# Two-block model on one core: the experts' gate and up products as three one-pass products of split operands, down weights loaded whole

## What is computed

```python
def hierarchical_moe(h, rg_w, rg_b, re_w, re_b, w_gate, w_up, w_down):
    ...  # combine[token, expert]: weight of the two chosen experts, else 0
    for e in range(N_EXPERTS):                                   # 16
        act = jax.nn.silu(hf @ w_gate[e]) * (hf @ w_up[e])       # 512x1024 @ 1024x512
        out = out + combine[:, e:e + 1] * (act @ w_down[e])      # 512x512 @ 512x1024
    return out.reshape(b, s, d)

def first_block(...):
    ...
    h2 = rmsnorm(x, norm2_g[l]) * (1.0 + scale2) + shift2
    y = hierarchical_moe(h2, ...)
    x = x + gate2 * y
    return rmsnorm(x, final_g)
```

## Time and profile before

| | us |
|---|---|
| median of 3 runs | 2555.88 |
| lowest to highest | 2555.7 to 2556.81 |
| the profiled execution | 2549.77 |
| its span in the trace | 2548.2 |

### The profile page before, as it was taken

One profiled execution on the slowest core, in us unless ns is written; L12 is line 12 of the kernel. 1 busy time (PEld: TensorE's weight loads), 2 busy tenths in 40 slices (PEclk: granted clock), 3 DMA queues, 4 the chain that ended last, 5 costly groups with the idle time before them and its releaser, 6 DMA issues.

```text
span 2548.2 us, 25617 instructions
## 1 busy us (share of the span) xinstructions
PE 2320.7 (91%) x9884; PEld 1662.4 (65%) x9884; DVE 1069.1 (42%) x1528; ACT 787.8 (31%) x1292; POOL 180.5 (7%) x222
## 2 busy tenths in 40 slices
PE   6899999979999995988879999989999997899998
PEld 4657666654444444874668888878865555788887
DVE  5635533351111115224554444453335544544444
ACT  3444521231010013210542123442344553311343
POOL 0330002010000001001000000001212200000000
PEclk9999899999999997978989999999989998999999
DMA  9304035728988884302023222233100001232221
GB/s 355 108 1 149 17 110 180 273 83 297 316 302 311 308 302 140 99 21 78 1 66 97 94 99 99 100 84 111 56 2 1 1 1 53 88 99 93 90 100 66
DMA packets 156367, 309.23 MB, mean 121 GB/s; under 512 B 18014, under 2 KB 19939, under 8 KB 156261
## 3 DMA queue, kind: packets, MB, share of 16 engines
q1 hardware_dynamic: 136308, 261.21, 30.2%
q0 software_dynamic: 11376, 41.42, 4.2%
q10 hardware_dynamic: 8580, 5.16, 0.8%
HBM read 276.56 MB, written 30.99 MB: 121 GB/s over the span
## 4 chain that ended last, share of the span: by engine, by line
PE 79%; DVE 10%; ACT 4%; issue 3%; DMA 2%; ACTq 1%; POOL 0%; DVEq 0%; POOLq 0%; SPq 0%; PEldq 0%
PE PB L1530 45%; PE PB L1933 8%; PE PB L1952 4%; PE PB L2212 3%; PE PB L1515 2%; PE PB L2188 1%; DVE WL L2306 1%; PE PB L1993 1%; PE PB L2016 1%; PE PB L2189 1%; DVE CI L3028 1%; PE PB L1756 1%; PE PB L2151 1%; DVE X L2366 1%; PE PB L1677 1%
## 5 line engine op out<-in xcount | busy, mean ns | idle before, releaser
L2306 DVE TENSOR_TENSOR WL<-RING,WH 128x1024 fp32r<-128x1024 f32 x232 | 286.3, 1234 | 662.0 <-ACT WH L892 385.6
L892 ACT CAST WH<-RING 128x1024 fp32r<-128x1024 f32 x232 | 243.4, 1049 | 873.8 <-PE PB L1530 849.2
L1530 PE MATMUL PB<-HTH,WH 128*128 128x512 f32 x1056 | 416.6, 395 | 16.0 <-DVE WL L2306 10.2
L1530 PE MATMUL PB<-HTL,WH 128*128 128x512 f32 x1056 | 413.8, 392 | 0.0
L1530 PE MATMUL PB<-HTH,WL 128*128 128x512 f32 x1056 | 413.2, 391 | 0.0
L1530 PEld LDWEIGHTS PB<-HTH,WH 128*128 128x128 f32 x1056 | 200.0, 189 | 61.8 <-DVE WL L2306 12.5
L1933 PE MATMUL PB<-RING,HT 128*128 128x512 f32 x512 | 226.3, 600 | 9.0 <-DVE HT L2782 5.7
L1530 PEld LDWEIGHTS PB<-HTH,WL 128*128 128x128 f32 x1056 | 199.9, 189 | 41.9
L1530 PEld LDWEIGHTS PB<-HTL,WH 128*128 128x128 f32 x1056 | 200.1, 190 | 41.5 <-issue 0.7
L1530 PE MATMUL PB<-WH,NHH 128*128 128x512 f32 x512 | 199.4, 389 | 1.8 <-DVE NHL L2309 1.8
L1530 PE MATMUL PB<-WH,NHL 128*128 128x512 f32 x512 | 199.2, 389 | 0.0
(11 more groups left out here) (489 smaller groups left out, 3266.0 us busy)
## 6 DMA issues: line engine op xcount, KB each, us to landing
RING<-in_mlp_w SPq DMA_DIRECT2D x64, 1024.0 KB, 5.1
RING<-in_expert_w_gate SPq DMA_DIRECT2D x32, 1024.0 KB, 5.5
RING<-in_expert_w_up SPq DMA_DIRECT2D x32, 1024.0 KB, 5.7
RING<-in_expert_w_down SPq DMA_DIRECT2D x32, 1024.0 KB, 6.7
BIG<-in_ada_w SPq DMA_DIRECT2D x10, 2048.0 KB, 10.8
RING<-in_w_in SPq DMA_DIRECT2D x20, 1024.0 KB, 5.1
dispatch_rows<-BIG POOLq DMA_DIRECT2D x24, 512.0 KB, 16.1
RING<-in_a_w_in SPq DMA_DIRECT2D x10, 1024.0 KB, 5.0
```

Of the source, the lines that this page charges most:

```text
L892: ins = nc.scalar.copy(WH[:, q % 2], halves_of(n, q))
L1530: yield pe.matmul(dst, lhs, rhs, start=(start and n == 0), stop=(stop_ and n == 2))
L2306: ins = V.tensor_tensor(WL[:, q % 2], halves_of(n, q), WH[:, q % 2].bitcast(F32), ALU.subtract)
```

## The change

It rewrites the gate and up products of the 16 experts in the way of the other stages, and keeps the down products in float32.

- Gate and up weights: the ring carries only these now, 64 chunks (`CH["moe"]` 96 to 64). Parts are cast and subtracted into `EWH` and `EWL`, four places each (`MOE_SLOTS`), which lie in the first half of `BIG`. The expert's rows are split too, into `XSH` and `XSL` (in `HTL`). An expert has 8 parts of 6 products, 48 one-pass products in place of 16 float32 ones.
- A ring place is free when VectorE has subtracted its second part (`low_ready`), no longer when TensorE has begun it.
- Down weights: ScalarE issues one load of 2 MB for each expert, 128 partitions by 4 whole rows of 1024 numbers, into two places of their own (`DNW`, in the second half of `BIG`). Each issue waits that the load before it has landed and, from expert 2 on, that the down products of two experts before are done.
- The loops are written out for 16 experts. Gate alternates between the banks `PB[2]` and `PB[7]`. The activations of expert e-1 are transposed within gate and up of expert e, after its third part; the rows of expert e+1 after its fifth.
- The final gain row goes to `QS`, since its place in `BIG` is taken.

```diff
-            with sp.Fori(0, EXPERTS // 4) as i:
-                for e in range(4):
...
-                    for d in DOWN_AFTER[e]:
-                        for half in range(2):
-                            load(CH["moe"] + DN_AT[d] + half, expert(a["expert_w_down"], d, 0, half * W),
-                                 turn=i, per_turn=24)
+            def expert(at_, w, e, k0, c0):
+
+                n = CH["moe"] + at_
+                sp.wait_ge(low_ready, part_no("wout", 2 * at_ + 2) if at_ < SLOTS else part_no("moe", 2 * (at_ - SLOTS) + 2))
+                sp.dma_start(slot(n), tall(w[0, e], k0, c0)).then_inc(arrived[n % SLOTS], 16)
...
@@ ScalarE
+            def expert_high(e, j):
+
+                q = 8 * e + j
+                act.wait_ge(arrived[(GU_AT[e] + j // 2) % SLOTS], slot_count(CH["moe"] + GU_AT[e] + j // 2))
+                if q >= MOE_SLOTS:
+                    act.wait_ge(part_begun, part_no("moe", q - MOE_SLOTS + 2))
+                nc.scalar.copy(EWH[:, q % MOE_SLOTS], halves_of(CH["moe"] + GU_AT[e] + j // 2, j)).then_inc(high_ready, 1)
...
+            def expert_down_weights(e):
+
+                act.wait_ge(expert_down_in, 32 + 16 * e)
+                act.dma_start(DNW[e % 2], a["expert_w_down"][0, e].rearrange("(t p) n -> p t n", p=P)).then_inc(expert_down_in, 16)
+
+            for e in range(2):
+                expert_down_weights(e)
...
+            for e in range(EXPERTS):
+                expert_high(e, 4)
+                if e > 1:
+                    act.wait_ge(down_done, e - 1)
+                    expert_down_weights(e)
+                expert_high(e, 5)
+                expert_high(e, 6)
+                expert_high(e, 7)
+                if e > 0:
+                    act.wait_ge(x_lo, e)
+                expert(e + 1, (e + 1) % 2)
+                if e + 1 < EXPERTS:
+                    expert_rows_high(e + 1)
+                    for j in range(3):
+                        expert_high(e + 1, j)
+                silu(e, e % 2)
+                if e + 1 < EXPERTS:
+                    expert_high(e + 1, 3)
...
@@ TensorE
+            def gate_up_split(e, after):
+
+                pe.wait_ge(x_lo, e + 1)
+                for j in range(8):
+                    q, bank = 8 * e + j, PB[(2, 7)[e % 2]] if j < 4 else PB[3]
+                    if j == 0 and e > 1:
+                        pe.wait_ge(silu_done, e - 1)
+                    if j == 4:
+                        pe.wait_ge(act_done, e + 1)
+                    pe.wait_ge(low_ready, part_no("moe", q + 1))
+                    w = (EWH[:, q % MOE_SLOTS], EWL[:, q % MOE_SLOTS])
+                    for k in range(2):
+                        for n, ins in enumerate(three(bank[:, :], w, k, (XSH[e % 2], XSL[e % 2]), 2 * (j % 4) + k, "N",
+                                                      slice(0, P), j % 4 == 0 and k == 0, j % 4 == 3 and k == 1)):
...
+                    if j in after:
+                        after[j]()
+                ins.then_inc(gu_done, 1)
...
+            for e in range(EXPERTS):
+                after = {4: lambda: rows_T(e + 1, (e + 1) % 2, (e + 1) // 2)}
+                if e > 0:
+                    after[2] = lambda: act_T(e - 1, (e - 1) % 2)
+                gate_up_split(e, after)
+                if e > 0:
+                    expert_down(e - 1, (lambda: act_T(e, e % 2)) if e == EXPERTS - 1 else None)
+            expert_down(EXPERTS - 1)
...
@@ VectorE
+            for e in range(EXPERTS):
+                expert_low(e, 4)
+                if e > 1:
+                    result(e - 2, e % 2, (e - 2) // 2)
+                expert_low(e, 5)
+                expert_low(e, 6)
+                expert_low(e, 7)
+                if e > 0:
+                    product_T(e - 1, (e - 1) % 2)
+                rows_T(e + 1, (e + 1) % 2)
+                if e + 1 < EXPERTS:
+                    rows_low(e + 1)
+                    for j in range(3):
+                        expert_low(e + 1, j)
+                product(e, e % 2)
+                if e + 1 < EXPERTS:
+                    expert_low(e + 1, 3)
```

More of the change, by code:

```diff
@@ L567, in _ @@
                 halves(CH["wout"] + 2 * half, a["w_out"][0], half * W)
-            with sp.Fori(0, EXPERTS // 4) as i:
-                for e in range(4):
[L571 to L576, removed]
-                    for d in DOWN_AFTER[e]:
-                        for half in range(2):
-                            load(CH["moe"] + DN_AT[d] + half, expert(a["expert_w_down"], d, 0, half * W),
-                                 turn=i, per_turn=24)
+            def expert(at_, w, e, k0, c0):
[3 more added lines that the diff above has]
+            for e in range(EXPERTS):
+                for m in range(4):
+                    expert(GU_AT[e] + m, a["expert_w_gate"] if m < 2 else a["expert_w_up"], e, KK * (m % 2), 0)
             sp.wait_ge(routed, 3)
@@ L1078, in _ @@
             upto(8)
+            def expert_high(e, j):
[4 more added lines that the diff above has]
+                nc.scalar.copy(EWH[:, q % MOE_SLOTS], halves_of(CH["moe"] + GU_AT[e] + j // 2, j)).then_inc(high_ready, 1)
+            for j in range(2):
+                expert_high(0, j)
             act.wait_ge(vec_t, 7)
@@ L1401, in rows_out @@
                 pool.dma_start(dst, YN[e % 2]).then_inc(y_out[e % 2], 16)
[L1403 to L1408 removed]
+            for e in range(EXPERTS):
+                rows_in(e + 1, (e + 1) % 2, 2, disp[(e + 1) * P:(e + 2) * P, :])
+                if e > 1:
+                    rows_out(e - 2, e % 2, back[(e - 2) * P:(e - 1) * P, :])
+            for e in range(EXPERTS - 2, EXPERTS):
+                rows_out(e, e % 2, back[e * P:(e + 1) * P, :])
             pool.wait_ge(routed, 3)
@@ L1943, in act_T, with down @@
                 ins.then_inc(a_tp, 1)
-            def down(E, e, weights, starts):
+            def down(E, e, weights, starts, between=None):
                 pe.wait_ge(a_ht, E + 1)
@@ L1949, in down @@
                 for m in range(2):
+                    if between is not None and m == 1:
+                        between()
                     w = weights(m)
@@ L1955, in down, with expert_down, chunk @@
                 ins.then_inc(down_done, 1)
[L1957 to L1972 removed]
+            def expert_down(e, between=None):
+                def chunk(m):
+                    if m == 0:
+                        pe.wait_ge(expert_down_in, 32 + 16 * (e + 1))
+                    return DNW[e % 2][:, :, m * W:(m + 1) * W]
+                down(e, e % 2, chunk, False, between)
+            first_rows_T()
+            for e in range(EXPERTS):
+                after = {4: lambda: rows_T(e + 1, (e + 1) % 2, (e + 1) // 2)}
[5 more added lines that the diff above has]
+            expert_down(EXPERTS - 1)
             pe.wait_ge(routed, 3)
@@ L2667, in _, with expert_low @@
             upto_wout(8)
+            def expert_low(e, j):
+                q = 8 * e + j
+                dve.wait_ge(high_ready, part_no("moe", q + 1))
+                V.tensor_tensor(EWL[:, q % MOE_SLOTS], halves_of(CH["moe"] + GU_AT[e] + j // 2, j),
+                                EWH[:, q % MOE_SLOTS].bitcast(F32), ALU.subtract).then_inc(low_ready, 1)
+            dve.wait_ge(low_ready, part_no("wout", 8))
+            for j in range(2):
+                expert_low(0, j)
             dve.wait_ge(aux_in, AUX["router"])
```

84 lines of the change are left out of this document (37 added, 47 removed).

## The result

| | before | after |
|---|---|---|
| median | 2556.35 us (4 runs, 2555.7 to 2558.78) | 2498.39 us (4 runs, 2496.54 to 2499.94) |
| the profiled execution | 2549.77 us | 2499.94 us |

The ratio is 0.9772, with a 95% interval of 0.9759 to 0.9785: 58 us faster. The forecast was 2503, in a range of 2494 to 2532.

The account below looks back on a forecast made before the run. TensorE was taken to bound the kernel, busy 91% of the span. The long stretch would fall 63 us (365.9 to 298.4 + 4.5 = 303), the start cost 10: 2555.9 - 53 = 2503 us, range 2494 to 2532.

Parts of the forecast that it names:

- What bounds the stage: Expert stage, second expert to last: TensorE bounds it, working 344.67 of 365.94 us; DMA 0.87 busy, loads early.
- The products: Gate and up of each expert: 48 one-pass products take 10.8 us in place of 13.90, 3.1 us less.
- The transpositions: Activations and next expert's rows, moved into gate and up: 1.64 us per expert, before and after.
- The gaps: TensorE's idle time before down products: moving transpositions removes the 15.6 us copy wait and most of the 21.3 us.
- Feeding the parts: Casts and subtractions per expert: VectorE 14.8 us, ScalarE 11.8, both fit a 19.4 us cycle; 0.3 us kept each, 4.5 in all.
- the rival from VectorE: Expert stage: VectorE at 76% delays row loads or parts, returning 15 to 30 us; 0.28 together with DMA rate.
- Before the stage: Four casts and subtractions of the first expert ahead of the stage are covered by waits: cost 0, uncovered 5 us.
- The start: First expert: ScalarE, held at the second down load, leaves TensorE idle 13 us; cost 10 us, bounds 6 and 15.
- The DMA rival: Expert stage: queues cannot sustain 373 GB/s, returning 10 to 22 us, 2513 to 2525 us; 0.28 together with VectorE.
- The rival's second reading: Whole expert stage before: 302 GB/s at share 0.87 means 347 at share 1, so an expert takes 21.2 us.
- The slow ring: Gate and up ring places refill too slowly; each us of landing over 12 paid per expert, about 2565 at 17; chance 0.06.
- The sum: Long stretch falls from 365.9 to 303 us, 63 less; with 10 lost at the start, the stage ends 53 us earlier.

Follow-up runs that it names:

- The float32 experiment: Changed kernel with gate and up as 16 float32 products of the high part in place of 48 one-pass products: 2538.6 us, ratio 0.9932 to before.
- its second profile: The changed kernel measured once more with nothing altered: 2497.82 us, ratio 0.9778 to before.

## Why the prediction came out

**What bounds the stage.** Right: TensorE led before and leads after, with 240.00 of 240 us busy. The rest is point by point.

**The products**, 46.5 us forecast for 15 experts. The float32 experiment gives 42: 2.8 us for an expert and not 3.1. The 48 one-pass products cost 0.227 us each (five triples, 15 products, from 649.68 to 653.09, take 3.41), 10.9 for the forecast's 10.8, and the 16 float32 ones 13.7 and not 13.90, by the tail named above. The whole cycle got shorter by 22.09 - 19.13 = 2.96 us, 44.4 for 15.

**The transpositions.** Taken at 1.64 us before and after. By distances of starts they took 1.38 before (633.37 to 634.75, above). Between one-pass products they add 0.46 and 0.89, 1.35 in all: the second row of each pair below comes one triple (0.68) and this much after the first.

```profile
653.09 0.40 PE L1574 MATMUL PB<-EWL,HTL 128*128 128x512 f32 x1
653.32 0.60 PE L2006 MATMUL PB<-IDENT,NAT 128*128 128x128 f32 x4
...
654.23 0.40 PE L1574 MATMUL PB<-EWL,HTL 128*128 128x512 f32 x1
...
656.29 0.39 PE L1574 MATMUL PB<-EWL,HTL 128*128 128x512 f32 x1
656.52 1.03 PE L1966 MATMUL PB<-IDENT,HT 128*128 128x128 f32 x8
...
657.86 0.39 PE L1574 MATMUL PB<-EWL,HTL 128*128 128x512 f32 x1
```

**The gaps.** The size was right, 19.8 of 21.3 us gone; the reason was not, so the size was right by luck. "Because both transpositions move into gate and up" fell with the experiment that moves them back and finds no wait. 9.4 us come from VectorE's copy ahead of the product, which one moved line does in the kernel before. The prediction counted the four waits ahead of a second down in a row (6.6) as the same wait and the three for the rows at a loop turn (5.7) as the same handoff; the moved line leaves both. They stand where a turn of the loop ends, and the loop is gone: after has one such place, its last two downs, with a wait of 1.43. That the unrolled order took them away is argued, not tried.

**Feeding the parts.** 4.5 us were kept for it, and none was needed: the 1.43 us idle of the long stretch stand before the last downs. VectorE works 14.1 us in a cycle and ScalarE 11.2 (14.8 and 11.8 forecast), and TensorE waits for no subtraction within the stretch. So the rival from VectorE did not come either: at 74% busy it cost TensorE nothing there. The reserve less this idle time is 3 of the 6.8 us by which the long stretch did better than forecast; the rest is busy time, 294.79 for 298.4, in the main the transpositions (15 x 0.29 = 4.4), against which the products cost 1.6 more than forecast. Only with two part places does the chain show, at about 1.3 us for most parts.

**Before the stage.** Cost 0 forecast. From the row at 523.25 to the first rows before took 48.8 us, after 49.4 and its second profile 48.8: within 1 us of the forecast.

**The start.** 10 us forecast, 12.2 in the profile. The mechanism was right to the row: the cast of part 4 behind the second down issue, 13.54 us of pause for "13 us of nothing". The prediction's working began with the first products at 3.8 us after the first rows; they came 3.9 after (580.82 - 576.93). TensorE resumed 24.8 us after, for 22.7: the scattering took 9.29 us of GpSimd's waiting where before had 7.36. The second expert began 33.9 us after the first rows, for 31.5. What the working did not ask is what the pause is worth: removing 9.1 us of it gave 6.4, and removing all of it no more, since the second expert's rows are late next.

**The DMA rival** failed by its price. TensorE's pace asked for 373 GB/s on end, and the rival held that the queues would not keep it up; the earlier trace rows had shown 385 to 395 for 10 us. The queues held 385 for 240 us, and 397 when asked for more. The Trainium skill, "DMA: Bandwidth & Descriptors", section Specifications, gives about 358 GB/s as a core's limit; both windows disagree, by 8 and 11%. The same page of the Trainium skill, section "Bandwidth", has the condition that the prediction overlooked: it gives 425 GB/s for 16 MB on a single core with the neighbour idle, and about 358 where both stream. The kernel runs on one core, and 385 and 397 lie between. The rival's second reading, 347 GB/s at a share of 1, came from dividing by a share of 0.87 in a stretch with idle queues, and fell with it. The argument by 4 KB rows was also empty: loads by halves of 2 KB cost nothing.

**The slow ring.** Landings did grow from 5.5 to 9.6 for gate and 13.2 for up, past the 12 us at which the prediction started to count:

```profile
RING<-in_expert_w_gate SPq DMA_DIRECT2D x24, 1024.0 KB, 9.6
...
RING<-in_expert_w_up SPq DMA_DIRECT2D x24, 1024.0 KB, 13.2
```

TensorE has no wait in the stretch that comes of it, where the prediction's price, each us over 12 once for an expert, would be 18 us. ScalarE shows some of it (40.3 us in 13 waits for gate loads, at most 3.7), which its slack of 8 us in a cycle absorbs. So the point from which it decides is above 13.2; where, wasn't tried.

**The sum.** Forecast -63 + 10 = -53; the profile has -69.7 + 12.2 = -57.5, so two misses partly cancel. The stage ends at 907.09 for 959.73, 52.6 us earlier, or 57.5 counted from the first rows; the prediction asked for 44. Of its other signs the pause of 12 to 14 us and the DMA rate above 360 GB/s came; the cycle of 19.13 us is shorter than its 19.4 to 19.8. Of the 69.7, 44.4 are 15 cycles shorter by 2.96, 19.8 idle time, and 3.6 two gate and ups of before that took 15.73 and 15.69 us for 13.90, with a mean granted clock of 0.72 and 0.73 in their first 6 us:

```profile
593.79 15.73 PE L1933 MATMUL PB<-RING,HT 128*128 128x512 f32 x32 [1.68 <-ACT HT L1108]
...
879.78 15.69 PE L1933 MATMUL PB<-RING,HT 128*128 128x512 f32 x32 [1.89 <-DVE HT L2782]
```

```profile
593.79:600.00 6.21, 6.21 (x11) 2.73 (x12) 0.00 (x0) 0.00 (x0) 0.00 (x0) 0.72 0.46 165
```

The last 1.9 us are about what an estimate gives for tails that are not hidden ahead of a wait: in before the two transpositions end after 1.47 us where they add 1.38 without a wait, twelve times, and the single one after 0.60 for 0.43, four times, 1.8 in all. The prediction's check of its sum, 344.9 for 344.67, was luck too: by distances of starts its groups come to about 339, and the two slow gate and ups and the open tails made up the rest.

## What to carry to other kernels

Take the cost of an instruction from the distance of two starts, not from a group's duration, which holds a tail that the next group hides. Before a gap is put down to where an instruction stands on the engine that waits, look in the list of the engine that is waited for: here one line of VectorE's list was worth 9 us without any of the rest. And a load that an engine issues after a wait stops that engine's compute too; price its removal by what is late next: here 9.1 us off a pause of 13.9 were worth 6.4, and taking the rest away no more.

## What was not expected

- DMA queues moved 385 GB/s over 240 us beside a TensorE that was busy all the time, and 397 when the products were fewer. At 385 loads of 1 MB landed in 10 to 13 us, and ScalarE's waits for them never reached TensorE.
- TensorE ran at full clock through the long stretch, but in the first expert, after waits of 4.6 to 13.9 us it began again at the lower of its two levels, 1.2 of 2.4 GHz: a pair of one-pass products took 1.19 us in place of 0.62. In the 20 us with the pause the granted clock was 0.70 in the mean. A wait as such does not settle it: in before, three gate and ups follow a wait of 1.89 us, and only that of 879.78 ran slowly.
- Two transpositions that stand together ahead of down cost about 0.1 us more in an expert than apart between one-pass products.
